# The second layer's long filters computed among the last four experts of the first layer

## The chip, the cores and the metric

The kernel runs on one core of a Trainium2 chip. Its time is the device time of one execution in microseconds (us); the median of three runs of the kernel before is 1987.41 us. TensorE is called PE here, VectorE DVE, ScalarE ACT, GpSimd POOL and SyncE SP.

## What is computed

A trunk of two layers over 256 tokens of width 1024, all in float32. A layer is a mixer and a mixture of experts:

```python
xn = rms_norm(x, norm1_w[l]); cols = xn @ w_in[l]
attn = mla_branch(...)                       # 16 heads
hy = hyena_branch(cols[..., COL_HYENA:COL_GATE], feats, tau, ...)
gates = sigmoid(cols[..., COL_GATE:])
merged = gates[:, :, 0] * (attn @ w_attn_branch[l]) + gates[:, :, 1] * (hy @ w_hyena_branch[l])
x = x + merged @ w_out[l]
x = x + expert_choice_ffn(rms_norm(x, norm2_w[l]), router_w[l], ...)   # 16 experts, 32 tokens each
```

The long filters of the Hyena branch do not depend on `x`, only on weights and positions, and this is what the change uses:

```python
h = sin(fr1 * (feats @ w1 + b1)); h = sin(fr2 * (h @ w2 + b2))
h = (h @ w3).reshape(L, 2, 1024) * exp(-tau * |deltas|)
h = h / sum(|h|, axis=0);  h_spec = rfft(h, n=2 * S, axis=0)
z = parts[0]
for n in range(2): z = parts[n + 1] * long_conv(z, h_spec[:, n], skip[n])
```

## The kernel before, in words

The program is written by hand for each engine; its order is the order of the code, and semaphores alone join the engines. Layers are `L` 0 and 1, experts `e` 0 to 15.

**Memory.** `ring` (22,528 columns of 4 bytes on 128 partitions) and `region` hold weights. In the mixer the ring has five slots (`SLOT_AT`) for 17 dense *units* of 2 MB: unit 0 the key and value up-projection, 1 to 6 the columns of the Hyena branch, 7 to 10 the gates, 11 to 14 the branch projections, 15 and 16 `w_out`. Units 14 to 16 lie in `R`, the first 12,288 columns of `region`. `m1` takes the latent weights, `m2` those of the query up-projection. In the experts the weights of one come in three transfers: A (6.5 MB: `w_gate` and the first part of `w_up`), B (5.0 MB: the rest of `w_up`) and D (5.8 MB: `w_down`). A has two areas (`wg_a`), one at the top of the ring and one in `region`, used by even and odd experts; B and D have one area each.

**SP** (`block.sync`) issues nearly all transfers in one queue. A transfer waits until the reader of what lies in its place is done: A waits for `gate_a` (the gate product of the expert two before, and one block of its up product), B for `up_done` and D for `o_psum` of the expert before. Whatever stands behind a waiting transfer waits too. ACT issues a few small loads in a queue of its own.

**PE in an expert** (`group`, L839): the gate product (L866), the up product (L866) in bank 3, transposes (L900, L906), the down product (L919), and four products (L937) that take the result to its tokens. In between ACT computes silu and DVE multiplies.

**The long filters** are computed in the mixer of each layer. The hidden layers (PE L519 and L537, DVE `sine_argument`, ACT Sin) lie in the query up-projection (L530). Behind the attention, between products for the gates (`next_gates`, L569), PE computes for each quarter `it` of the filters `filter_time` (L632, two products), `filter_spectrum` (L645, four) and `filter_sum` (L655, four). DVE (`decayed`), ACT (`abs_h`, `odd_filter`) and POOL take part in each. Then z is transposed (L669) and taken to its spectrum (`to_spectrum`, L681).

Of the kernel before, what the change touches and what calls it, by code (L numbers as in the profile page):

```python
# [51 lines left out]
NU, RING, RING_UNITS = 17, 5, 14  # L52
SLOT_AT = (0, 4096, 9856, 13952, 18176)
SLOT = DB * FF
# [11 lines left out]
def unit_slot(n):  # L66
    return (n + 4) % RING
# [7 lines left out]
UNITS_IN_SLOT = [sum(unit_slot(n) == s for n in range(RING_UNITS)) for s in range(RING)]  # L75
# [33 lines left out]
def build(nc, x, vecs, fvecs, qkw_in, consts_in, decay_in, w_lat, w_q_b, units_in,  # L109
          filt12, filt3, w_ga, w_gbu, w_down, w_down_last, out):  # L110
    with ExitStack() as ctx:
# [38 lines left out]
        w3 = R[:, 8192:8192 + 2048]  # L150
        w12 = R[0:64, 10240:10432]
        h2T = R[:, 10432:10432 + P]
        h1T = R[0:64, 10688:10688 + S]
        rr = R[0:64, 10944:10944 + 768]
        habs = R[:, 10688:11712]
        spec = R[:, 0:8192].rearrange("p (n b c) -> p n b c", n=2, b=4)
# [7 lines left out]
        decay = region[:, 12 * 1024:12 * 1024 + 2048].rearrange("p (b c) -> p b c", b=SB)  # L164
        hflt = W[:, 0:2048].rearrange("p (h b c) -> p h b c", h=2, b=SB)
# [49 lines left out]
        m2 = ring[:, M2AT:M2AT + QB * NH * QK].rearrange("p (i c) -> p i c", i=QB)  # L215

        def unit(n):
            if n >= RING_UNITS:
                return R[:, (n - RING_UNITS) * UNIT:(n - RING_UNITS + 1) * UNIT]
            a = SLOT_AT[unit_slot(n)]  # L220
            return ring[:, a:a + UNIT]

        def unit8(n):
            return unit(n).rearrange("p (i c) -> p i c", i=DB)

        wkv = unit(0).rearrange("p (i c) -> p i c", i=KVB)
# [8 lines left out]
        names = """one_dve half_dve consts_in dft_in vec_in fvec_in qkw_in filt_in decay_in wqb_in wgbu_in wga_third_in wga_last_in wu_tail_in out_done  # L235
# [16 lines left out]
        unit_in = [sem(f"unit_in{i}") for i in range(RING)]  # L252
        late_in = [sem(f"late_in{i}") for i in range(NU - RING_UNITS)]
# [4 lines left out]
        def _(sp):  # L258
            for L in range(DEPTH):
# [13 lines left out]
                if L == 0:  # L273
                    for t in range(SB):
                        sp.dma_start(x3[:, t], x[0, t * P:(t + 1) * P]).then_inc(x_in[t], 16)
                else:
                    sp.wait_ge(s["post_dve"], L * 4 + FREE)
                    sp.dma_start(vec[:, :], vecs[L]).then_inc(s["vec_in"], 16)
# [6 lines left out]
                sp.dma_start(unit(1), units_in[L, 1]).then_inc(unit_in[unit_slot(1)], 16)  # L285
                sp.dma_start(m2, w_q_b[L].rearrange("(i p) c -> p i c", p=P)).then_inc(s["wqb_in"], 16)
                sp.dma_start(unit(0), units_in[L, 0]).then_inc(unit_in[unit_slot(0)], 16)
# [5 lines left out]
                sp.dma_start(fvec[:, :], fvecs[L]).then_inc(s["fvec_in"], 16)  # L293

                def load_gate_a(e):
                    sp.dma_start(wg_a[e % 2], w_ga[L * E + e]).then_inc(wga_in[e % 2], 16)
# [28 lines left out]
                for n in range(2, RING_UNITS):  # L325
                    if n == 3:
                        sp.wait_ge(s["q_psum"], (L + 1) * 6)
                    if n >= RING:
                        unit_is_used(n - RING)
                    sp.dma_start(unit(n), units_in[L, n]).then_inc(unit_in[unit_slot(n)], 16)  # L330
                for k, (reader, count) in enumerate((("prod_dve", 2), ("prod_dve", 4), ("prod_dve", 4))):
                    sp.wait_ge(s[reader], L * 4 + count)
                    sp.dma_start(unit(RING_UNITS + k), units_in[L, RING_UNITS + k]).then_inc(late_in[k], 16)


                unit_is_used(9)
                unit_is_used(10)
# [9 lines left out]
                for b in range(FB):  # L347
                    unit_is_used(RING_UNITS + b)
# [7 lines left out]
                load_gate_a_second(12 * 1024 + SPARE, REGION - 3072)  # L356
                for e in range(1, E):
# [6 lines left out]
                    elif e < E - 2:  # L364
                        sp.wait_ge(s["gate_a"], L * E + e)
                        load_gate_a(e + 1)
                    elif e == E - 1:
# [3 lines left out]
                    if e == E - 2:  # L371
# [3 lines left out]
                    if e < E - 1:  # L375
                        load_down(e)
                    else:
# [11 lines left out]
        def _(pool):  # L389
            for L in range(DEPTH):  # L390
# [25 lines left out]
                for it in range(4):  # L416
                    pool.wait_ge(s["habs_act"], L * 4 + it + 1)
                    nc.gpsimd.tensor_tensor(habs[:, 0:HW], habs[:, 0:HW], habs[:, HW:2 * HW],
                                            ALU.add).then_inc(s["habs_pool"], 1)
# [3 lines left out]
        def _(pe):  # L423
# [3 lines left out]
            def unit_arrived(L, n):  # L427
                if n >= RING_UNITS:
                    pe.wait_ge(late_in[n - RING_UNITS], 16 * (L + 1))
                else:  # L430
                    pe.wait_ge(unit_in[unit_slot(n)], 16 * (L * UNITS_IN_SLOT[unit_slot(n)] + n // RING + 1))

            for n in ("gate_done", "up_done", "o_psum"):
                pe.sem_inc(s[n], FREE)
            def unread(count):
                for _ in range(count):
                    mm(bank(7, S), late[:, 0:P], late[:, 0:S], start=True, stop=True)

            pe.wait_ge(s["half_dve"], 1)
            unread(5)  # L440
            for L in range(DEPTH):
# [57 lines left out]
                def half_block(b, k):  # L499
                    n, j = 1 + b // 4, b % 4  # L500
                    for i in range(4 * k, 4 * k + 4):
                        m = mm(bank(b % 2, S), unit8(n)[:, i, j * P:(j + 1) * P], xnT[:, i],  # L502
# [7 lines left out]
                for i in range(5):  # L510
# [6 lines left out]
                pe.wait_ge(s["dft_in"], 16)  # L517
                pe.wait_ge(s["filt_in"], 48 * (L + 1))
                mm(bank(7, S), w12[0:33, 0:P], cst[0:33, C_FEAT:C_FEAT + S],  # L519
                   start=True, stop=True).then_inc(s["filt_psum"], 1)  # L520
# [4 lines left out]
                for g in range(6):  # L525
# [3 lines left out]
                    for i in range(QB):  # L529
                        m = mm(bank((3 + g) % 7), latT[:, i, t * P:(t + 1) * P], m2[:, i, c * 512:(c + 1) * 512],  # L530
                               start=i == 0, stop=i == QB - 1)
                    m.then_inc(s["q_psum"], 1)
                    if g == 1:

                        pe.wait_ge(s["consts_in"], 16)
                        pe.wait_ge(s["sin_act"], 2 * L + 1)
                        mm(bank(7, S), w12[:, 64:64 + P], h1T, start=True, stop=True).then_inc(s["filt_psum"], 1)  # L537

                unit_arrived(L, 0)
                for g in range(8):  # L540
# [26 lines left out]
                def gate_product(i, g, dst):  # L567
                    for k in range(DB):
                        m = mm(dst, unit8(7 + 2 * (i // 4) + g)[:, k, i % 4 * P:(i % 4 + 1) * P], xnT[:, k],  # L569
# [54 lines left out]
                def filter_time(it):  # L624
                    n, c = it // 2, it % 2
                    if it == 0:
                        pe.wait_ge(s["sin_act"], 2 * L + 2)
                    else:
                        pe.wait_ge(s["h_dve"], L * 4 + it)
                    for t in range(SB):  # L630
                        k = slice(64 * t, 64 * (t + 1))
                        m = mm(bank(t), h2T[k], w3[k, n * D + c * HW:n * D + (c + 1) * HW], start=True, stop=True)  # L632
# [1069 lines left out]
```

## Time and profile before

| | us |
|---|---|
| median of 3 runs (lowest, highest) | 1987.41 (1987.09, 1988.1) |
| span of the profiled execution, first to last instruction | 1985.9 |
| mixer of layer 1 and up to the first expert's end | 0 to about 411 |
| experts of layer 1 | about 411 to 996 |
| mixer of layer 2 and up to the first expert's end | about 996 to 1398 |
| experts of layer 2 | about 1398 to 1986 |
| PE busy (share of the span) | 1565.1 (79%) |
| DVE, ACT, POOL busy | 564.8, 289.5, 45.7 |
| bytes over the span | 644.37 MB, mean 324 GB/s |

The span leaves 1.5 us of the median outside. In both mixers PE is busy without a break and the DMA engines are partly idle; in the experts it is the other way round: the transfers come back to back and PE waits for them twice in each expert. The granted clock of TensorE is full in the mixers and 0.8 on average in the experts.

### The profile page before, as it was taken

To read this page: it belongs to the slowest core of one execution; us is meant where nothing else is said; L and a number is where in the kernel's file an instruction comes from. 1 tells how busy PE (TensorE), PEld (TensorE's weight loads), DVE (VectorE), ACT (ScalarE), POOL (GpSimd) and SP (SyncE) were. 2 spreads that over 40 slices of the span, in tenths; PEclk is the share of its full clock that TensorE was granted. 3 is DMA by queue.
4 is the path that set the end of the run, shared out by engine and by line. 5 is a ranking of instruction groups with operands and counts; after the bars stand their busy time and mean duration, and the time that the engine had idled before them with its cause. 6 is when DMAs were issued, how large, how long until landed. Compare 5 with 4: busy or idle time off the path is not lost.

```text
span 1985.9 us, 22283 instructions
## 1 busy us (share of the span) xinstructions
PE 1565.1 (79%) x9646; PEld 876.6 (44%) x9646; DVE 564.8 (28%) x1108; ACT 289.5 (15%) x610; POOL 45.7 (2%) x24
## 2 busy tenths in 40 slices
PE   9999999876665666576799999999766566666767
PEld 6687688532221232132267877885222222222322
DVE  3654772211111111111136547712111112111211
ACT  3233210210000000000032432102100000000010
POOL 0300000000000000000002000000000000000000
PEclk9999999998877887788899999998888778877888
DMA  8622055699999999999956221546999999999998
GB/s 296 233 86 85 1 226 214 252 417 434 431 428 438 428 433 433 429 433 425 426 209 233 85 85 44 235 178 271 439 427 432 435 430 431 431 433 432 430 430 343
DMA packets 26987, 644.37 MB, mean 324 GB/s; under 512 B 2960, under 2 KB 3984, under 8 KB 6672
## 3 DMA queue, kind: packets, MB, share of 16 engines
q1 hardware_dynamic: 25840, 638.47, 76.4%
q10 hardware_dynamic: 1056, 4.53, 0.8%
q8 instruction: 76, 1.25, 0.3%
q14 instruction: 15, 0.12, 0.0%
HBM read 641.94 MB, written 1.05 MB: 324 GB/s over the span
## 4 chain that ended last, share of the span: by engine, by line
DMA 49%; PE 48%; DVE 1%; DVEq 1%; issue 1%; ACT 0%; SPq 0%; ACTq 0%
DMA region<-w_down_dram 44%; PE ps L919 11%; PE ps L502 7%; PE ps L569 6%; PE ps L709 6%; DMA region<-w_down_last_dram 3%; PE ps L767 3%; DMA consts<-consts_dram 2%; PE ps L530 2%; PE ps L692 1%; PE ps L645 1%; PE ps L592 1%; PE ps L547 1%; PE ps L681 1%; PE ps L866 1%; PE ps L616 1%
## 5 line engine op out<-in xcount | busy, mean ns | idle before, releaser
L866 PE MATMUL ps<-ring,region 128*32 128x384 f32 (+1 forms) x2944 | 297.1, 538 | 190.9 <-DMA ring<-w_gbu_dram 190.9
L919 PE MATMUL ps<-region,late 128*32 128x512 f32 x1320 | 215.8, 777 | 157.7 <-DMA region<-w_down_dram 156.5
L866 PEld LDWEIGHTS ps<-ring,region 128*32 128x32 f32 x2944 | 122.2, 124 | 359.7 <-DMA ring<-w_gbu_dram 211.7
L919 PEld LDWEIGHTS ps<-region,late 128*32 128x32 f32 x1320 | 57.5, 138 | 295.1 <-issue 293.4
L502 PE MATMUL ps<-xnT,ring 128*128 128x256 f32 x768 | 178.3, 380 | 4.3 <-DVE region L1209 2.6
L1570 DVE TENSOR_TENSOR region<-region,ps 128x256 f32<-128x256 f32 x32 | 13.5, 421 | 543.7 <-PE ps L866 543.7
L502 PEld LDWEIGHTS ps<-xnT,ring 128*128 128x128 f32 x768 | 140.6, 190 | 23.9 <-DVE region L1209 4.4
L937 PE MATMUL ps<-region 128*128 128x512 f32 x256 | 123.8, 615 | 24.0 <-issue 22.4
L1581 DVE COPY region<-ps 128x512 f32<-128x512 f32 x32 | 22.1, 692 | 358.8 <-PE ps L919 358.1
L569 PE MATMUL ps<-xnT,ring 128*128 128x256 f32 x512 | 115.8, 380 | 0.0
L1584 DVE TENSOR_TENSOR x<-x,ps 128x512 f32<-128x512 f32 x128 | 88.0, 687 | 76.3 <-PE ps L937 76.3
L569 PEld LDWEIGHTS ps<-xnT,ring 128*128 128x128 f32 x512 | 95.9, 190 | 18.2 <-issue 6.3
L866 PE MATMUL ps<-region 128*32 128x384 f32 (+1 forms) x1152 | 96.1, 463 | 0.3 <-DMA region<-w_ga_dram 0.2
L937 PEld LDWEIGHTS ps<-region 128*128 128x128 f32 x256 | 40.9, 188 | 109.5 <-issue 66.7
L1180 ACT ACT_TABLE_LOAD x30 | 38.5, 1283 | 329.2 <-PE ps L866 329.2
L709 PE MATMUL ps<-region,ring 128*128 128x256 f32 x384 | 84.5, 379 | 0.0
L1189 ACT ACTIVATE region<-ps 128x512 f32<-128x512 f32 x32 | 19.1, 597 | 405.6 <-PE ps L919 392.1
L709 PEld LDWEIGHTS ps<-region,ring 128*128 128x128 f32 x384 | 72.8, 190 | 9.8
L866 PEld LDWEIGHTS ps<-region 128*32 128x32 f32 x1152 | 41.7, 109 | 55.8 <-issue 49.1
L1184 ACT ACTIVATE region<-ps 128x256 f32<-128x256 f32 x32 | 12.3, 384 | 364.0 <-PE ps L900 364.0
L767 PE MATMUL ps<-region 128*128 128x512 f32 x128 | 56.4, 593 | 0.0
L1061 ACT ACTIVATE region<-ps,small 128x256 f32<-128x256 f32 x64 | 29.8, 470 | 84.4 <-DVE small L1363 84.4
(207 smaller groups left out, 1478.1 us busy)
## 6 DMA issues: line engine op xcount, KB each, us to landing
region<-w_down_dram SPq DMA_DIRECT2D x28, 5632.0 KB, 32.5
ring<-w_gbu_dram SPq DMA_DIRECT2D x30, 4928.0 KB, 33.3
region<-w_ga_dram SPq DMA_DIRECT2D x12, 6336.0 KB, 37.1
ring<-w_ga_dram SPq DMA_DIRECT2D x12, 6336.0 KB, 34.7
ring<-units_dram SPq DMA_DIRECT2D x28, 2048.0 KB, 8.6
region<-units_dram SPq DMA_DIRECT2D x6, 2048.0 KB, 11.8
region<-w_ga_dram SPq DMA_DIRECT2D x2, 4928.0 KB, 32.1
ring<-w_ga_dram SPq DMA_DIRECT2D x2, 4288.0 KB, 13.6
```

The lines of the kernel that those rows point to most:

```text
L502: m = mm(bank(b % 2, S), unit8(n)[:, i, j * P:(j + 1) * P], xnT[:, i], start=i == 0, stop=i == DB - 1)
L530: m = mm(bank((3 + g) % 7), latT[:, i, t * P:(t + 1) * P], m2[:, i, c * 512:(c + 1) * 512], start=i == 0, stop=i == QB - 1)
L569: m = mm(dst, unit8(7 + 2 * (i // 4) + g)[:, k, i % 4 * P:(i % 4 + 1) * P], xnT[:, k], start=k == 0, stop=k == DB - 1)
L709: m = mm(bank(2 * (i % 2) + 1, S, g * S), unit8(n)[:, k, j * P:(j + 1) * P], (uT if g else aT)[:, k], start=k == 0, stop=k == DB - 1)
L767: m = mm(bank(4 + 2 * t + c), mT[:, k, t * P:(t + 1) * P], unit8(15 + c)[:, k], start=k == 0, stop=k == DB - 1)
L866: m = mm(bank(b, QW[j], rows=CAP, row0=CAP * j), xs[:, i, q * CAP:(q + 1) * CAP], w[i][:, j * FT:j * FT + QW[j]], start=i == 0, stop=i == ...
L919: m = mm(bank(c, rows=CAP, row0=CAP * j), hT[:, b * P + CAP * j:b * P + CAP * (j + 1)], wd[:, CT * b + j, c * 512:(c + 1) * 512], start=b ...
L937: mm(bank(6 + k % 2), gselT[:, t * P:(t + 1) * P], o_sb[:, c * 512:(c + 1) * 512], start=True, stop=True).then_inc(s["y2_psum"], 1)
L1061: m = af(p_t[:, h % 2, t], bank(3 + h % 2, S, t * S), ACT.Exp, bias=nmax[:, c:c + 1], accum_out=rsum[:, c:c + 1])
L1180: af(sil[:, 0:2 * P], bank(2, 2 * P), ACT.Silu)
L1581: copy(o_sb[:, 512:1024], bank(1)).then_inc(s["o_dve"], 1)
L1584: tt(xc, xc, bank(6 + k % 2), ALU.add).then_inc(s["x_dve"], 1)
```

## The change

Layer 1 keeps its filters where they were. Those of layer 2 are computed while the experts 12 to 15 of layer 1 run, in seven steps `k` (`filter_ahead`): 0 and 1 are the hidden layers, steps 2 to 5 begin with `filter_time(k - 2)`, steps 3 to 6 have `filter_spectrum` and `filter_sum` of quarter `k - 3`. On PE an even step lies behind the gate product, before the first block of the up product, and an odd step behind the transposes, before the down product. Expert 12 has steps 0 and 1, 13 has 2 and 3, 14 has 4 and 5, and 15 has 6.

```diff
+                        if last and L < DEPTH - 1:
+                            filter_ahead(L + 1, ahead[0], n)
                         pe.wait_ge(s["hid_dve"], n + FREE)
-                        product(3, wu[q % 2], 0).then_inc(s["gate_a"], 1)
+                        product(3, wu[home], 0).then_inc(s["gate_a"], 1)
...
+                        if last and L < DEPTH - 1:
+                            if q < GROUP - 1:
+                                filter_ahead(L + 1, ahead[1], n)
+                            filter_banks_read(L + 1, min(ahead[1], 6))
                         pe.wait_ge(s["hT_dve"], n + 1)
...
+            def filter_ahead(L, k, n):
+                if k == 0:
+                    pe.wait_ge(s["x_dve"], n * 4 + X_FREE)
+                if k < 2:
+                    filter_hidden(L, k)
+                    return
+                if k < 6:
+                    if k >= 4:
+                        pe.wait_ge(s["spec_dve"], L * 12 + 3 * (k - 4) + 2)
+                    filter_time(L, k - 2)
+                if k >= 3:
+                    it = k - 3
+                    pe.wait_ge(s["x_dve"], n * 4 + X_FREE)
+                    filter_spectrum(L, it, 0, 6)
+                    if k < 6:
+                        pe.wait_ge(s["h_dve"], L * 4 + it + 2)
+                    filter_spectrum(L, it, 1, 0)
+                    pe.wait_ge(s["gselT_act"], n + k % 2)
+                    filter_sum(L, it, 4, S)
+            def filter_banks_read(L, k):
+                if k == 1:
+                    pe.wait_ge(s["arg_dve"], 2 * L + 2)
+                else:
+                    pe.wait_ge(s["spec_dve"], L * 12 + 3 * (k - 3) + 2)
```

On DVE the even step stands before the multiplication that the down product needs, and on ACT four experts are now written out behind the loop. ACT loads what the filters need in its own queue: the hidden weights (48 KB) and `vec` (64.5 KB) once the rows of the last group are picked, the output weights (512 KB) and the decay (1024 KB) in expert 12. Before, these loads but `vec` were made in the mixer, with the output weights twice.

```diff
 # DVE, group
+                        if last and L < DEPTH - 1:
+                            filter_ahead(L + 1, 2 * q)
                         dve.wait_ge(s["sil_act"], n + 1 + FREE)
                         dve.wait_ge(s["up_done"], n + 1 + FREE)
 # DVE, filter_ahead, step 0
+                if k == 0:
+                    dve.wait_ge(s["vec_in"], 16 * (L + 1))
 # ACT, behind the loop over twelve experts
+                    act.wait_ge(s["xs_psum"], 4 * NG * (L + 1))
+                    act.wait_ge(s["post_dve"], (L + 1) * 4 + FREE)
+                    load_filter_hidden(L + 1)
+                    act.dma_start(vec[:, :], vecs[L + 1]).then_inc(s["vec_in"], 16)
 # ACT, expert 12, behind silu
+                        filter_ahead(L + 1, ahead[0])
+                        if ahead[0] == 0:
+                            act.wait_ge(s["gate_a"], n + 1)
+                            load_filter_out(L + 1)
+                            load_decay(L + 1)
```

The filters and their spectra lie in the upper part of the ring. So from expert 13 of layer 1 on there is one area for A, that in `region`:

```diff
-                    elif e < E - 2:
+                    elif e < (E - 2 if last_layer else E - 3):
                         sp.wait_ge(s["gate_a"], L * E + e)
                         load_gate_a(e + 1)
...
                     if e < E - 1:
                         load_down(e)
+                        if not last_layer and e >= E - 3:
+                            sp.wait_ge(s["gate_a"], L * E + e + 1)
+                            load_gate_a(e + 1)
```

The mixer of layer 2 has three slots of the ring for its units, and three places in `R`; the query weights lie in `region`.

```diff
+UNIT_HOMES = ((4, 0, 1, 2, 3, 4, 0, 1, 2, 3, 4, 0, 1, 2, 5, 6, 7),
+              (1, 0, 2, 1, 0, 2, 1, 0, 2, 5, 6, 1, 0, 2, 5, 6, 7))
+UNIT_ORDER = ((2, 3, 4, 5, 6, 7, 8, 9, 10, 11, 12, 13, 14, 15, 16),
+              (2, 3, 4, 5, 6, 7, 8, 11, 9, 10, 12, 13, 14, 15, 16))
```

SP's queue at the end of layer 1 and the start of layer 2, from B of expert 13 on, before:

```order
L299 DMA ring<-w_gbu_dram 128x9856 [waits up_done]
L319 DMA region<-w_down_dram 128x11264 [waits o_psum]
L299 DMA ring<-w_gbu_dram 128x9856 [waits up_done]
L312 DMA region<-w_ga_dram 128x2816 [waits gate_a]
L319 DMA region<-w_down_dram 128x11264 [waits o_psum]
L312 DMA region<-w_ga_dram 128x9856
L316 DMA ring<-w_gbu_dram 128x5632 [waits up_done]
L316 DMA ring<-w_gbu_dram 128x4224
L380 DMA region<-w_down_last_dram 128x5632 [waits o_psum]
```

and now:

```order
L325 DMA ring<-w_gbu_dram 128x9856 [waits up_done]
L345 DMA region<-w_down_dram 128x11264 [waits o_psum]
L322 DMA region<-w_ga_dram 128x12672 [waits gate_a]
L325 DMA ring<-w_gbu_dram 128x9856 [waits up_done]
L345 DMA region<-w_down_dram 128x11264 [waits o_psum]
L322 DMA region<-w_ga_dram 128x12672 [waits gate_a]
L342 DMA ring<-w_gbu_dram 128x5632 [waits up_done]
L342 DMA ring<-w_gbu_dram 128x4224
L418 DMA region<-w_down_last_dram 128x5632 [waits o_psum]
```

A of expert 14, which stood ahead of these rows, now stands behind D of expert 13, and A of 15 is whole and behind D of 14. PE in the mixer of layer 2 behind the attention, before (L569 are the gates, L669 transposes z, L681 is the spectrum of z):

```order
L569 MATMUL ps<-xnT,ring 128x256 x8
L632 MATMUL ps<-region 128x512 x2
L569 MATMUL ps<-xnT,ring 128x256 x8
L632 MATMUL ps<-region 128x512 x2
L645 MATMUL ps<-region,consts 96x512 x4
L655 MATMUL ps<-consts,region 128x1 x4
...
L669 MATMUL ps<-consts,region 128x128 x8
L645 MATMUL ps<-region,consts 96x512 x4
L669 MATMUL ps<-consts,region 128x128 x8
L655 MATMUL ps<-consts,region 128x1 x4
L569 MATMUL ps<-xnT,ring 128x256 x8
L681 MATMUL ps<-region,consts 96x512 x4
```

and now (L680 the gates, L746 the transposes, L759 the spectrum of z):

```order
L680 MATMUL ps<-xnT,ring 128x256 x8
L746 MATMUL ps<-consts,region 128x128 x8
L680 MATMUL ps<-xnT,ring 128x256 x8
L746 MATMUL ps<-consts,region 128x128 x8
L680 MATMUL ps<-xnT,ring 128x256 x8
L759 MATMUL ps<-region,consts 96x512 x4
```

The four quarters of the filters are gone from here. Their products now stand in the experts; expert 13, behind its transposes (L994, L1000) and before its down product (L1017):

```order
L994 MATMUL ps<-consts,region 128x128 x2
L1000 MATMUL ps<-consts,region 128x128 x2
L1000 MATMUL ps<-consts,region 128x96
L503 MATMUL ps<-ring 128x512 x2
L515 MATMUL ps<-ring,consts 96x512 x4
L523 MATMUL ps<-consts,xnT 128x1 x4
L1017 MATMUL ps<-region,late 32x512 x22
```

where L1000 was followed by L1017 before.

## Rows read from the trace of the kernel before

**Rows 1.** The page: busy tenths and GB/s in 40 slices of the span
```profile
PE   9999999876665666576799999999766566666767
PEclk9999999998877887788899999998888778877888
GB/s 296 233 86 85 1 226 214 252 417 434 431 428 438 428 433 433 429 433 425 426 209 233 85 85 44 235 178 271 439 427 432 435 430 431 431 433 432 430 430 343
```

**Rows 2.** Chain of waits, end of layer 1: start, us, what
```profile
891.89 32.60 DMA region<-w_down_dram
...
960.61 27.64 DMA region<-w_down_last_dram
```

**Rows 3.** Chain of waits, layer 2 behind the attention
```profile
1179.52 1.06 PE ps L632 x4
...
1185.29 3.60 PE ps L645 x8
1188.89 0.79 PE ps L655 x8
...
1201.62 3.43 PE ps L645 x8
1205.06 0.95 PE ps L669 x8
...
1206.79 3.56 PE ps L569 x16
1210.35 3.43 PE ps L681 x8
```

**Rows 4.** Windows: busy us of each engine, granted clock, DMA share, GB/s
```profile
1175.00:1215.00 40.00, 40.00 (x167) 23.94 (x164) 20.19 (x39) 15.09 (x22) 5.05 (x4) 1.00 0.04 19
```

**Rows 5.** Timeline, PE, query up-projection of layer 2
```profile
1025.42 5.39 PE L530 MATMUL ps<-ring,region 128*128 128x512 f32 x12 [0.18 <-ACT region L1027]
1030.79 0.67 PE L537 MATMUL ps<-region 64*128 64x256 f32 x2
```

**Rows 6.** DMA issues from 995 to 1062 us: size of one, us to landing
```profile
ring<-units_dram SPq DMA_DIRECT2D x3, 2048.0 KB, 7.5
region<-filt_dram ACTq DMA_DIRECT2D x2, 512.0 KB, 14.0
region<-decay_dram ACTq DMA_DIRECT2D x1, 1024.0 KB, 4.8
region<-filt_dram ACTq DMA_DIRECT2D x1, 48.0 KB, 8.9
```

**Rows 7.** Timeline, PE, expert 12 of layer 1
```profile
860.95 6.01 PE L866 MATMUL ps<-ring,region 128*32 128x384 f32 x72
871.20 6.41 PE L866 MATMUL ps<-ring,region 128*32 128x384 f32 x56 [4.25 <-DMA ring<-w_gbu_dram]
884.62 7.23 PE L919 MATMUL ps<-region,late 128*32 128x512 f32 x44 [5.67 <-DMA region<-w_down_dram]
892.60 3.86 PE L937 MATMUL ps<-region 128*128 128x512 f32 x8 [0.75 <-issue]
```

**Rows 8.** Timeline, DVE, first sine argument of layer 2, its first and last row
```profile
1027.09 0.53 DVE L1217 TENSOR_SCALAR region<-ps,vec 64x256 f32<-64x256 f32 x1
...
1029.90 0.28 DVE L1228 TENSOR_SCALAR region<-region 64x256 f32<-64x256 f32 x1
```

**Rows 9.** Timeline, SP's queue: issues of B and of D of expert 13
```profile
877.68 0.33 SPq L299 DMA_DIRECT2D ring<-w_gbu_dram  x1
891.89 0.33 SPq L319 DMA_DIRECT2D region<-w_down_dram  x1
```

**Rows 10.** Timeline, PE: expert 14 without a wait; the first down product of layer 2
```profile
936.87 10.52 PE L866 MATMUL ps<-ring,region 128*32 128x384 f32 x128
...
1397.75 5.35 PE L919 MATMUL ps<-region,late 128*32 128x512 f32 x44 [0.62 <-DVE late L1574]
```

**Rows 11.** Timeline, PE, last products of layer 1
```profile
988.28 1.92 PE L945 MATMUL ps<-region,late 128*32 128x512 f32 x16 [0.34 <-DMA region<-w_down_last_dram]
993.91 1.98 PE L937 MATMUL ps<-region 128*128 128x512 f32 x4 [0.80 <-DVE region L1581]
```

**Rows 12.** Timeline, SP, layer 2: A and B of the first expert
```profile
1281.76 0.33 SPq L302 DMA_DIRECT2D ring<-w_ga_dram  x1
1309.49 0.33 SPq L299 DMA_DIRECT2D ring<-w_gbu_dram  x1
```

More of the change, by code:

```diff
@@ L51 @@
 UNIT = DB * 512
[L52 removed]
 SLOT_AT = (0, 4096, 9856, 13952, 18176)
+RING = len(SLOT_AT)
+ROWS_HOMES = 3
 SLOT = DB * FF
@@ L414, in _ @@
                     ALU.mult).then_inc(s["qkr_pool"], 1)
[L416 to L419, printed above, removed]
+                if L == 0:
+                    sum_of_halves(0)
+                if L < DEPTH - 1:
+                    sum_of_halves(L + 1)
         @block.tensor
@@ new lines, in filter_time @@
+            def filter_time(L, it):
+                n, c = it // 2, it % 2
+                if it == 0:
+                    pe.wait_ge(s["filt3_in"], 32 + 16 * L)
+                    pe.wait_ge(s["sin_act"], 2 * L + 2)
+                else:
+                    pe.wait_ge(s["h_dve"], L * 4 + it)
+                for t in range(SB):
+                    k = slice(64 * t, 64 * (t + 1)) if L == 0 else slice(0, 64)
+                    h = h2T[L][k] if L == 0 else h2T[L][:, t * P:(t + 1) * P]
+                    m = mm(bank(t), h, w3[L][k, n * D + c * HW:n * D + (c + 1) * HW], start=True, stop=True)
+                m.then_inc(s["f3_psum"], 1)
@@ new lines, in basis, with filter_spectrum @@
+            def basis(par, f):
+                a = C_F + (2 * par + f) * NK
+                return cst[:, a:a + NK]
+            def filter_spectrum(L, it, f, bank0):
+                pe.wait_ge(s["h_dve"], L * 4 + it + 1)
+                if it >= 1:
+                    pe.wait_ge(s["spec_dve"], L * 12 + 3 * (it - 1) + f + 1)
+                for par in range(2):
+                    m = mm(bank(bank0 + par, rows=NK), basis(par, f), hflt[L][it % 2][:, par], start=True, stop=True)
+                m.then_inc(s["dft_psum"], 1)
@@ new lines, in filter_sum @@
+            def filter_sum(L, it, b, off):
+                pe.wait_ge(s["habs_pool"], L * 4 + it + 1)
+                if it >= 1:
+                    pe.wait_ge(s["spec_dve"], L * 12 + 3 * it)
+                for j in range(4):
+                    m = mm(bank(b, 1, off + j), habs[L][:, j * P:(j + 1) * P], ones, start=True, stop=True)
+                m.then_inc(s["hsum_psum"], 1)
+            def filter_ahead(L, k, n):
[17 more added lines that the diff above has]
+                    filter_sum(L, it, 4, S)
@@ L1214, in sine_argument @@
                 dve.wait_ge(s["filt_psum"], 2 * L + k + 1)
-                a, turns, rest = (rr[:, i * S:(i + 1) * S] for i in range(3))
+                a, turns, rest = (rr[L][:, i * S:(i + 1) * S] for i in range(3))
                 c = V_FB1 + 2 * k
```

419 lines of the change are left out of this document (241 added, 178 removed).

## The prediction

> **What bounds the kernel now.** I read the slices first [rows 1]. In slices 1 to 7 and 21 to 27, the mixers, PE stands at 9 and the DMA engines move 1 to 250 GB/s in most slices; in the other slices they move 425 to 438 GB/s and PE stands at 6 or 7. So the mixers are PE's and the experts are the transfers'. The chain of waits says the same: it goes from each D to the next [rows 2], 40 us for an expert. An expert's 17.3 MB at 432 GB/s take 40.1 us: A 15.0, B 11.7, D 13.4. In the mixer of layer 2 the chain is PE alone, and in the stretch of the filters PE is busy for 40.00 of 40 us at full clock, while DVE has 20.19 and the DMA engines 4% [rows 3, 4]. PE time taken from there should come off the end, as nothing else is near to full. PE time added to the experts should cost nothing until PE is late with freeing a weight area that the next transfer waits for, and bytes added there cost in full.
>
> **What is taken away.** The filters' products go from the chain of layer 2 [rows 3]: four times L632 at 1.06 (4.2), four times L645, three at 3.60 and one at 3.43 (14.2), four times L655 at 0.79 (3.2): 21.6 us. Checked the other way: from 1179.52 to 1210.35 there are 30.8 us, of which two gate products (3.65 and 3.56) and two transposes (1.05 and 0.95) stay, 9.2; again 21.6. ACT and POOL wait for nothing new there, and DVE's next work is released by L681, which moves along. The hidden layers: L537 stands between back-to-back products, and its chain share is 0.6; L519 was hidden, as L530 behind it waited for ACT anyway [rows 5]. Together **-22.2 us**. Layer 1's mixer computes the same in the same order: 0.
>
> **What is added in bytes.** 48, 512 and 1024 KB move from a stretch with idle DMA engines to one that has none: 1.62 MB at 432 GB/s, **+3.7 us**. `vec` (64.5 KB) was already loaded there.
>
> **What is moved in the experts.** Here a wait can appear, and I follow the clock of the profile through expert 12.
> - ACT issues the two small loads when the rows of the last group are picked, at about 861 [rows 7]. Each gives a DMA engine 4 and 8 rows, and each engine still has SP's rows of some 45 KB, 1.7 us each at 27 GB/s. The same 48 KB load took 8.9 us among SP's smaller rows, more than the 1024 KB decay took alone (4.8) [rows 6]; so such a load does not overtake. If one of SP's rows goes between every two, 12 rows need 20 us and start-up, and `vec` lands at about 884.5. The bounds: 8.9 us as measured (871), and the end of all that SP has queued, A no longer among it (897).
> - By the Trainium skill (DMA: Bandwidth & Descriptors, Queues, rings and completion order) an engine drains a whole packet of typically 9 to 17 descriptors before it turns to another ring. The two loads would then stand behind the rest of B and behind D of expert 12, and `vec` would land at 885 and the sum grow by about 0.5 us; no row before shows the order of single packets.
> - DVE waits for `vec` before the first sine argument, and the multiplication for the down product is queued behind it. An argument takes 3.1 us [rows 8]: 887.6. Multiplication, transposes and ACT's sine take it to about 890.5; the second hidden product (0.7) and the second argument, for which PE waits (`filter_banks_read`), take it to 894.7. The down product of expert 12 then starts at 895 in place of 884.62, and is cold as before (7.2 us): 902.3. So D of expert 13 is issued at 902.3 in place of 891.89 [rows 9].
> - Without A of expert 14, which the change moves behind it, the DMA engines have at that time only B of 13 (884.5 + 11.7) and ACT's 3.7 us: they run dry at 899.9. With 2 us from issue to data (a unit lands 7.5 us after issue for 4.9 us of bytes [rows 6], 2.6 for both ends) D flows from 904.3. **+4.4 us** idle. The bounds are 0 (`vec` before 880) and 15 (`vec` at 897 and a cold PE).
> - Expert 13: tokens 4.6, gate product and first block 6.0 [rows 7], step 2 1.1: 914. A of 14 is issued then, data from 916, and D ends at 917.7. 1.7 us to spare, so the single area for A costs 0 here, but only just. I take **+0.5**.
> - Step 3 has 5.5 us of products [rows 3] and some 1.6 us of hand-overs to ACT and DVE; up product 4.6 and down product 5.35 at full clock [rows 10]. D of 14 is issued at 933 and needed at 942, A of 15 at 950 and needed at 956. No wait of the transfers.
> - Expert 15: A lands at 973 and PE is free at 973.5; gate 5.3, step 6 4.4, up 5.3, hand-overs 3.2: the last down product starts at 991.5, when its first part lands. What follows is set by the last parts, as before: the chain ends in a transfer and two token products [rows 2, 11]. PE has about 2 us to spare, the only slack from here back to the start of expert 13's down product.
>
> **Layer 2's dense units.** Three slots serve while a slot is read for 12 us or more and a unit lands in 7.5 us [rows 6]: 0. The query weights are last in the first batch and need `o_psum` of the last expert; I have them 20 us after it, with L530 30 us after it. Units 9 and 10 land some 16 us after the attention, with 20 us to spare. Units 14 to 16 now wait for the last gate product and take 14.6 us, A of the first expert (before at 1281.76) another 10, and B is due at 1309.49 [rows 12]: 25 of 27.7 us. Costs 0; the gap that covers it is nearly used up.
>
> **Sum.** -22.2 + 3.7 + 4.4 + 0.5 = -13.6. From the span of 1985.9: 1972.3. The median is 1.5 us above the span, so the runs should give **1974 us**. A measurement of this kernel can tell about 0.2%, 4 us, from no change.
>
> **The rivals.**
> - *All side work hidden* (chance 0.20). `vec` lands early, as 8.9 us would have it, and only the bytes cost: 1987.4 - 22.2 + 3.7 = 1969. For it: the load is small. Against: rows 6.
> - *Long hand-overs* (0.14). Steps 3 to 6 have each two or three turns PE to ACT to DVE and back; 2 us more in each of four steps are 8, less the 2 of slack: 1980. The bank and table switches there are in no row before.
> - *A late load in layer 2* (0.05). If the query weights or units 14 to 16 are 10 us later than I have them, PE stands still in the mixer: 1984.
> - *The single area at half clock, slower than before* (0.06). PE's products in experts 13 to 15 could run at 1.2 GHz, as the down product of 12 does (7.2 against 5.35 us [rows 7, 10]). Steps 3 to 6 have about 21 us of products, which would take as much again; what is beyond the 2 us of slack goes to the end: 1974 + 19 = 1993. It decides from 15 us on. For it: the granted clock is 0.8 on average in the experts. Against: PE is cold there since it waits for B and D; from expert 13 on both are there before PE asks, and expert 14 of the kernel before, which waits for nothing, runs 128 products in 10.52 us. The Trainium skill (TensorE: Matmul & The Clock Gate, The HAM clock gate) has half the clock as the default, released by activity, which speaks for this rival only where PE stands still.
> - That the saving is none, because something other than PE holds layer 2, has nothing for it [rows 4].
>
> **How the numbers follow.** My forecast has 0.55. Of its cases all are faster by over 0.2% (below 1983.4), and so are the first two rivals; the third lies within 0.2% or just beyond. Faster 0.87, same 0.07, slower 0.06. The range goes from below the first rival, 1967, to beyond the second, 1982; the last two rivals and the tail of the bound of 15 us are left out.
>
> **What would show it.** In the profile after: the stretch between the attention and the first spectrum of z in layer 2 is 9 us, not 31; layer 1 ends some 8 us later; B of 13 and D of 13 have a gap of about 4 us of idle DMA between them and DVE's sine argument waits for a transfer into `vec`; the down product of expert 12 starts near 895; L1017 in experts 13 and 14 takes 5.4 us. Wrong: a DMA gap in front of A of 14 or of 15, half-clock products in steps 3 to 6, or PE waiting for units in layer 2.

## The result and the profile after

| | us (lowest, highest) | runs |
|---|---|---|
| before, same chip | 1987.74 (1987.09, 1988.1) | 4 |
| the change | 1975.55 (1974.04, 1978.51) | 4 |

The ratio is 0.994, 95% interval 0.9928 to 0.9952: 12.2 us less, where 13.4 were predicted. The profiled execution is the slowest of the four (span 1976.1, its run 1978.51); the other three have spans of 1972.2 to 1974.0. So some numbers of this profile are up to 4 us on the late side, and I give a second profile of the same kernel (`c1_change_again`, span 1972.5) where that matters. The slices, which answer to [rows 1]:

```profile
PE   9999999876655675658989999998757566556767
PEclk9999999998878787788999999999988788887888
GB/s 298 232 88 86 1 220 222 254 410 429 428 434 430 433 430 436 426 394 393 432 325 85 86 105 188 106 305 266 433 437 432 430 431 431 431 437 431 430 426 342
```

PE is fuller in slices 19 and 20, the last experts of layer 1 (8 and 9 tenths for 6 and 7), and in slices 18 and 19 the transfers fall to 394 and 393 GB/s, the one place among layer 1's experts where they are disturbed.

**Layer 2 gained what was forecast.** Timeline of PE behind the attention, for the stretch of [rows 3]:

```profile
1191.12 1.11 PE L746 MATMUL ps<-consts,region 128*128 128x128 f32 x8
1192.07 3.62 PE L680 MATMUL ps<-xnT,ring 128*128 128x256 f32 x16
1195.52 1.11 PE L746 MATMUL ps<-consts,region 128*128 128x128 f32 x8
1196.47 3.62 PE L680 MATMUL ps<-xnT,ring 128*128 128x256 f32 x16
1199.93 3.60 PE L759 MATMUL ps<-region,consts 128*96 128x512 f32 x8
```

From 1191.12 to the first spectrum of z at 1199.93 there are 8.8 us, where there were 30.8. Taken from the last product of layer 1 to the end of the span, it is 1976.1 - 1008.5 = 967.6 us, and was 1985.9 - 995.9 = 990.0: -22.4 for a forecast of -22.2.

**Layer 1 gave part of it back.** Its last products, which answer to [rows 11]:

```profile
994.39 2.77 PE L1043 MATMUL ps<-region,late 128*32 128x512 f32 x22 [2.16 <-DMA region<-w_down_last_dram]
999.20 3.62 PE L1043 MATMUL ps<-region,late 128*32 128x512 f32 x16 [2.04 <-DMA region<-w_down_last_dram]
...
1006.52 1.98 PE L1035 MATMUL ps<-region 128*128 128x512 f32 x4 [0.80 <-DVE region L1750]
```

The end of layer 1 moved from 995.9 to 1008.5, by 12.6 us (forecast 8.6). -22.4 + 12.6 is the whole difference of the spans, -9.8. The same rows in the second profile:

```profile
997.43 1.92 PE L1043 MATMUL ps<-region,late 128*32 128x512 f32 x16 [2.04 <-DMA region<-w_down_last_dram]
...
1003.06 1.98 PE L1035 MATMUL ps<-region 128*128 128x512 f32 x4 [0.80 <-DVE region L1750]
```

There the end moved by 9.1 us, and the products that the last transfer releases take 1.92 instead of 3.62: the granted clock from 999 to 1003 was 0.57 in the first profile, so mostly 1.2 GHz, and 1.00 (2.4 GHz) from 997.4 to 999.4 in the second.

Where it went is seen in expert 12. Timeline of PE, for [rows 7]:

```profile
861.77 5.36 PE L952 MATMUL ps<-ring,region 128*32 128x384 f32 x64
874.68 1.19 PE L486 MATMUL ps<-consts,xnT 33*128 33x256 f32 x2 [7.55 <-DMA xnT<-filt_dram]
875.80 7.33 PE L952 MATMUL ps<-ring,region 128*32 128x384 f32 x64
...
889.09 0.85 PE L1000 MATMUL ps<-consts,region 128*128 128x128 f32 x3 [5.59 <-DVE region L1738]
889.87 1.22 PE L491 MATMUL ps<-xnT 64*128 64x256 f32 x2
894.27 8.32 PE L1017 MATMUL ps<-region,late 128*32 128x512 f32 x44 [3.19 <-DVE xnT L1374]
```

DVE stood still for `vec`, as forecast:

```profile
885.40 0.53 DVE L1363 TENSOR_SCALAR xnT<-ps,vec 64x256 f32<-64x256 f32 x1 [22.58 <-DMA vec<-vecs_dram]
```

and SP's queue, for [rows 9]:

```profile
883.20 0.33 SPq L325 DMA_DIRECT2D ring<-w_gbu_dram  x1
902.65 0.33 SPq L345 DMA_DIRECT2D region<-w_down_dram  x1
915.26 0.33 SPq L322 DMA_DIRECT2D region<-w_ga_dram  x1
...
933.96 0.33 SPq L345 DMA_DIRECT2D region<-w_down_dram  x1
950.96 0.33 SPq L322 DMA_DIRECT2D region<-w_ga_dram  x1
...
971.36 1.28 SPq L418 DMA_DIRECT2D region<-w_down_last_dram  x3
```

There are two waits. One I had not priced: PE stands 7.55 us for the 48 KB of hidden weights and runs the up product at 7.33 us, the slow kind. So B of expert 13 is issued at 883.20, not at 877.68 [rows 9]. The other is the forecast one: the down product starts at 894.27 (forecast 895), and D of 13 is issued at 902.65 (902.3). The windows show what the DMA engines did in 5 us each; the last two columns are their busy share and their GB/s:

```profile
875.00:880.00 5.00, 5.00 (x33) 2.05 (x35) 0.00 (x0) 0.00 (x0) 0.00 (x0) 0.52 0.86 369
880.00:885.00 5.00, 3.50 (x40) 1.24 (x32) 0.00 (x0) 0.00 (x0) 0.00 (x0) 1.00 0.70 238
...
890.00:895.00 5.00, 1.81 (x6) 0.57 (x10) 3.14 (x8) 0.52 (x2) 0.00 (x0) 0.50 1.00 358
895.00:900.00 5.00, 5.00 (x28) 1.18 (x24) 0.00 (x0) 0.00 (x0) 0.00 (x0) 0.50 0.91 255
900.00:905.00 5.00, 4.24 (x24) 1.18 (x16) 1.20 (x2) 0.60 (x1) 0.00 (x0) 0.97 1.08 354
```

The gap before B of 13 is plain (share 0.70). Behind 890 it is different: the engines are busy, but move only 358, 255 and 354 GB/s. Something that flows there is slow. ACT issues the 512 KB at 888.54 and the decay at 889.07. Over the experts 12 to 15 (845 to 1000) the mean is 405 GB/s and was 427: 3.4 MB, or 7.9 us at 432 GB/s, are missing, and with the added 3.7 us of bytes that is 11.6 of the 12.6 us by which layer 1's end moved. Issues from 860 to 905, size and us to landing:

```profile
ring<-decay_dram ACTq DMA_DIRECT2D x1, 1024.0 KB, 16.0
ring<-filt_dram ACTq DMA_DIRECT2D x1, 512.0 KB, 14.5
vec<-vecs_dram ACTq DMA_DIRECT2D x1, 64.5 KB, 23.0
xnT<-filt_dram ACTq DMA_DIRECT2D x1, 48.0 KB, 12.7
```

### The profile page after: what moved, and what is told of

It reads as the page before. It is cut to its first block, busy times and chain, and to the rows that moved or that the text cites. A ratio compares the mean times of both kernels' runs of the same rounds, so it can differ in the third digit from the quotient of the medians.

```text
span 1976.1 us, 22283 instructions
## 1 busy us (share of the span) xinstructions
PE 1564.4 (79%) x9646; PEld 876.0 (44%) x9646; DVE 566.1 (29%) x1108; ACT 283.3 (14%) x604; POOL 45.8 (2%) x24
## 3 DMA queue, kind: packets, MB, share of 16 engines
HBM read 641.42 MB, written 1.05 MB: 325 GB/s over the span
## 4 chain that ended last, share of the span: by engine, by line
PE 50%; DMA 45%; DVE 2%; issue 1%; DVEq 1%; ACT 0%; SPq 0%; ACTq 0%
DMA region<-w_down_dram 40%; PE ps L1017 11%; PE ps L617 7%; PE ps L680 6%; PE ps L787 6%; PE ps L853 3%; DMA region<-w_down_last_dram 3%; PE ps L952 2%; DMA consts<-consts_dram 2%; PE ps L643 2%; PE ps L770 1%; PE ps L703 1%; PE ps L658 1%; PE ps L759 1%; PE ps L515 1%; DMA vec<-vecs_dram 1%
## 5 line engine op out<-in xcount | busy, mean ns | idle before, releaser
L952 PE MATMUL ps<-ring,region 128*32 128x384 f32 (+1 forms) x2872 | 287.8, 534 | 174.9 <-DMA ring<-w_gbu_dram 174.9
L1017 PE MATMUL ps<-region,late 128*32 128x512 f32 x1320 | 218.0, 785 | 145.7 <-DMA region<-w_down_dram 138.9
L1017 PEld LDWEIGHTS ps<-region,late 128*32 128x32 f32 x1320 | 57.5, 140 | 285.6 <-issue 277.4
L617 PE MATMUL ps<-xnT,ring 128*128 128x256 f32 x768 | 178.3, 380 | 4.3 <-DVE region L1355 2.6
L617 PEld LDWEIGHTS ps<-xnT,ring 128*128 128x128 f32 x768 | 140.6, 190 | 23.9 <-DVE region L1355 4.4
L1750 DVE COPY region<-ps 128x512 f32<-128x512 f32 x32 | 22.1, 692 | 342.5 <-PE ps L1017 341.9
L952 PE MATMUL ps<-region 128*32 128x384 f32 (+1 forms) x1224 | 102.7, 463 | 0.0
L680 PE MATMUL ps<-xnT,ring 128*128 128x256 f32 x384 | 86.8, 380 | 0.0
L680 PEld LDWEIGHTS ps<-xnT,ring 128*128 128x128 f32 x384 | 71.9, 190 | 13.5 <-issue 4.6
```

The lines of the kernel that those rows point to most:

```text
L617: m = mm(bank(b % 2, S), unit8(L, n)[:, i, j * P:(j + 1) * P], xnT[:, i], start=i == 0, stop=i == DB - 1)
L680: m = mm(dst, unit8(L, 7 + 2 * (i // 4) + g)[:, k, i % 4 * P:(i % 4 + 1) * P], xnT[:, k], start=k == 0, stop=k == DB - 1)
L952: m = mm(bank(b, QW[j], rows=CAP, row0=CAP * j), xs[:, i, q * CAP:(q + 1) * CAP], w[i][:, j * FT:j * FT + QW[j]], start=i == 0, stop=i == ...
L1017: m = mm(bank(c, rows=CAP, row0=CAP * j), hT[:, b * P + CAP * j:b * P + CAP * (j + 1)], wd[:, CT * b + j, c * 512:(c + 1) * 512], start=b ...
L1750: copy(o_sb[:, 512:1024], bank(1)).then_inc(s["o_dve"], 1)
```

## The experiments

The loss (9.6 us by medians: the 22.1 of `e7_no_filters` below, less the 12.5 of `c1_change_again`, each against the kernel before that stood beside it) has four candidates: the waits for the small loads, the added bytes, PE's products in the experts, and the single area for A. Theory A of the quotes is my sum: mostly the waits. The kernel before stood beside each batch: 1987.85 for c1 and e1 to e3, 1988.47 for e4 to e7, 1987.64 for the others. Differences are of medians; with each taken against the kernel before of its own batch they shift by up to 0.7. All but e4, e7, p1 and p2 are edits of the changed kernel.

**c1: the change again.** 

> The changed kernel once more, beside the three edits of it that follow. All theories: 1975.5 us within 2, and layer 1's last token products (L1035) end 10 to 13 us later than before.

1975.38 us, ratio 0.9939 (0.9926 to 0.9953). The result repeats. Layer 1 ends 9.1 us later than before in its profile, not 10 to 13. Where a profile of the change is compared with another run below, this one is the fairer.

**e1: `vec` before the twelve experts.**

```diff
+                    act.wait_ge(s["post_dve"], (L + 1) * 4 + FREE)
+                    act.dma_start(vec[:, :], vecs[L + 1]).then_inc(s["vec_in"], 16)
                     with act.Fori(0, SPARE_FROM) as e:
...
                     load_filter_hidden(L + 1)
-                    act.dma_start(vec[:, :], vecs[L + 1]).then_inc(s["vec_in"], 16)
```

> ACT loads vec of layer 2 ahead of the experts of layer 1; the 48 KB of hidden weights stay where the change has them. Theory A (the experts lose time because PE and DVE wait for the two small loads, which come late among SP's large rows): DVE's first sine argument starts when PE gives it (about 875), the down product of expert 12 at about 888 in place of 894, but PE still waits for the hidden weights until about 874 and B of expert 13 is issued late; 1972.5 us (1971 to 1974). Theory B (the added products and hand-overs, or the single area for A, cost the time): 1975.5. Theory C (only the bytes count, the waits are hidden): 1975.5.

1974.92, ratio 0.9933 (0.992 to 0.9947): not different from c1, a miss for A. The down product of expert 12 starts at 888.17, as expected, and D of 13 is issued at 896.17, 4.4 us earlier than in c1. Nearly nothing of that reaches the end: the last part lands only 1.6 us earlier (its 16 products start at 995.84, in c1 at 997.43), and these products take 3.59 us here and 1.92 there, so that layer 1 ends at 1005.1 in both profiles.

**e2: both small loads early.** The hidden weights go to a place that is free (`qkw`).

```diff
-        w12 = (R[0:64, 10240:10432], xnT_t[0:64, 0:192])
+        w12 = (R[0:64, 10240:10432], qkw[0:64, 0:192])
...
                     act.wait_ge(s["post_dve"], (L + 1) * 4 + FREE)
+                    load_filter_hidden(L + 1)
+                    act.dma_start(vec[:, :], vecs[L + 1]).then_inc(s["vec_in"], 16)
+                    with act.Fori(0, SPARE_FROM) as e:
+                        expert(e, False)
```

> Both small loads ahead of the experts of layer 1; the hidden weights of layer 2 go to the tile of qkw, which is free there. Theory A: no wait for either; B of 13 is issued at 878 and D of 13 by 893, no idle DMA engines, only the 3.7 us of bytes stay: 1969 us (1967 to 1970.5). Theory B and theory C: 1975.5.

1974.43, ratio 0.9932 (0.9918 to 0.9945), where A had 1969. Both waits are gone, and 1 us is gained. PE's timeline of e2 says what stands in their place:

```profile
889.26 8.10 PE L1017 MATMUL ps<-region,late 128*32 128x512 f32 x44 [9.90 <-DMA region<-w_down_dram]
```

D of expert 12, there at 884.62 in the kernel before [rows 7], now lands at 889. Its windows:

```profile
870.00:875.00 5.00, 3.93 (x34) 1.86 (x37) 1.34 (x4) 0.42 (x1) 0.00 (x0) 0.66 1.01 433
875.00:880.00 5.00, 3.91 (x37) 1.56 (x29) 1.68 (x4) 0.39 (x1) 0.00 (x0) 1.00 1.04 327
880.00:885.00 5.00, 0.00 (x0) 0.00 (x0) 2.11 (x6) 0.42 (x1) 0.00 (x0) 0.62 0.98 278
885.00:890.00 5.00, 0.74 (x4) 0.23 (x8) 0.00 (x0) 0.00 (x0) 0.00 (x0) 0.50 1.04 424
```

No gap (shares 1.04 and 0.98), and yet 327 and 278 GB/s in the 10 us that begin 3.4 us behind the issue of the 512 KB at 871.61. When the 1024 KB of the decay flow behind them, the rate is back at 424. The packets of e2, summed by queue (`--dma` with a window), say the same: from 875 to 884.4 an engine moves, while busy, 17.7 GB/s in ACT's rows and 18.8 in SP's beside them; from 884.4 to 902 it is 25.5 and 25.9. The queue and the size of the rows are the same in both stretches, and SP's large rows lie between them in both, so it is neither the second queue nor the mixing of small rows with large ones. So the slow loads and the waits overlap in the change: part of the slow stretch lies in time that the waits had lost already. That is my reading of why taking the waits away gives so little.

**e3: only the hidden weights early.** Their place is `qkw` as in e2, and `vec` stays where it was.

```diff
+                    act.wait_ge(s["post_dve"], (L + 1) * 4 + FREE)
+                    load_filter_hidden(L + 1)
                     with act.Fori(0, SPARE_FROM) as e:
...
-                    load_filter_hidden(L + 1)
                     act.dma_start(vec[:, :], vecs[L + 1]).then_inc(s["vec_in"], 16)
```

> Only the hidden weights early, vec stays late. Theory A: B of 13 is issued in time (878), but DVE still waits for vec until about 885 and the down product of expert 12 starts at about 894; the first gap of the DMA engines goes, a second of 3 to 4 us comes in front of D of 13: 1974 us (1972.5 to 1975.5). If the wait for the hidden weights alone were the cost, 1969; if neither counts, 1975.5.

1972.93, ratio 0.9925 (0.9911 to 0.9938), within what was expected, but not by the path expected: without the 48 KB ahead of it `vec` takes 17.6 us and lands near 878, not 885, the down product of expert 12 starts at 887.11, not 894, and of the second gap only a share of 0.86 in one window of 5 us is seen. Its median is 2.5 us below c1, but the intervals overlap.

**e4: the single area alone,** on the kernel before.

```diff
+        def second_home(L, e):
+            return e % 2 == 1 or (L < DEPTH - 1 and e == E - 2)
...
-                    elif e < E - 2:
+                    elif e < (E - 2 if last_layer else E - 3):
...
+                        if not last_layer and e >= E - 3:
+                            sp.wait_ge(s["gate_a"], L * E + e + 1)
+                            load_gate_a(e + 1)
```

> The kernel before with one part of the change alone: one area for A from expert 13 of layer 1 on, in SP's new order; filters and units as before. Theory A: A of 14 and of 15 are issued before the DMA engines run dry, no cost: ratio 1.000 (within 1 us). Theory B (the single area is what costs): 3 to 9 us slower than before.

1987.96, ratio 0.9995 (0.9986 to 1.0004). The single area costs nothing that can be measured.

**e5: few bytes.** e2, with 1/32 of the output weights and of the decay loaded for layer 2.

```diff
-                        act.dma_start(w3[M][64 * t:64 * (t + 1)], filt3[M]).then_inc(s["filt3_in"], 16)
+                        act.dma_start(w3[M][64 * t:64 * (t + 1), 0:(2048 if M == 0 else 64)], filt3[M][:, 0:(2048 if M == 0 else 64)]).then_inc(s["filt3_in"], 16)
...
-                    act.dma_start(decay[M], decay_in).then_inc(s["decay_in"], 16)
+                    act.dma_start(decay[M] if M == 0 else decay[M][:, :, 0:32], decay_in if M == 0 else decay_in[:, :, 0:32]).then_inc(s["decay_in"], 16)
```

> As e2_both_early, but the output weights and the decay of layer 2 are loaded only in 1 of 32 parts of their columns (the rest of the filters is computed from what lies there). Prices the bytes: the 1.57 MB at the rate of the experts are 3.6 us, so 3.5 us faster than e2_both_early (about 1965). If the small rows cost more than their bytes, 5 to 6 us faster; if they are hidden, the same as e2_both_early.

1967.33, ratio 0.9896 (0.9881 to 0.9911): 7.1 us less than e2 (7.7 against the kernel before of each), more than any of the three cases expected, where the bytes at 432 GB/s are 1.52 MB, 3.5 us. The two intervals together leave about 3 to 11 us for this difference, so the medians alone don't exclude the bytes' price; the rates in the windows are the firmer evidence. The same windows as in e2 read:

```profile
875.00:880.00 5.00, 4.45 (x44) 1.74 (x34) 1.20 (x4) 0.38 (x1) 0.00 (x0) 1.00 1.08 430
880.00:885.00 5.00, 0.00 (x0) 0.00 (x0) 2.58 (x7) 0.42 (x1) 0.00 (x0) 0.66 0.95 408
```

In e2 these 10 us moved 302 GB/s on average: 10 x (1 - 302 / 432) = 3.0 us lost. 3.5 + 3.0 is 6.5 of the 7.1. The run prices the 512 KB and the decay together, and not each.

**e6: the spectrum products twice.** e2 with 14.4 us of PE work more in experts 13 to 15:

```diff
-                for par in range(2):
+                for par in (range(2) if L == 0 else (0, 1, 0, 1)):
```

> As e2_both_early, with every product of filter_spectrum of layer 2 computed twice: 3.6 us more of PE in each of steps 3 to 6. Theory A has PE time in experts 12 to 15 hidden while the transfers are ahead: with both small loads early the slack at the last expert is 2 us and the 4 to 8 us regained, so of the 14.4 us some 5 to 8 come through. If PE were the bound there, all 14.4; if PE time is free, none.

1980.81, ratio 0.9967 (0.9955 to 0.9979): 6.4 us more than e2. PE's work in the experts of e2 is hidden, with some 8 us to spare.

**e7: the kernel before without layer 2's filters,** neither loads nor products nor DVE's and ACT's part:

```diff
-                filter_time(0)
...
-                filter_sum(3)
+                if L == 0:
+                    filter_time(0)
...
+                else:
+                    z_transposed(0)
+                    next_gates()
+                    z_transposed(1)
```

> The kernel before without any long filters in layer 2: their products, sines and loads are left out, and the spectra are what lies in their place. Prices what the change takes from the mixer: 22.2 us faster than before (1965.5), and 9 us from the attention to the first spectrum of z. If DVE or ACT hold the mixer behind it, less: 15 to 20 us.

1966.39, ratio 0.989 (0.9875 to 0.9906): -22.1 us, for a forecast of -22.2. This is what a perfect hiding place would give.

**p1 and p2: what extra bytes cost in either queue.** The kernel before, with 640 KB of constants (128 partitions, rows of 5 KB) loaded four times more in layer 1's experts, by ACT or by SP:

```diff
+                        if e in (4, 6, 8, 10):
+                            act.wait_ge(s["dft_in"], 8 * e - 16)
+                            act.dma_start(cst[:, C_F:C_N], consts_in[:, C_F:C_N]).then_inc(s["dft_in"], 16)
```

> The kernel before, with 4 loads of 640 KB (constants that it has already) added among the experts of layer 1 in ACT's queue. 2.62 MB at 432 GB/s are 6.1 us. Theory M (small rows of one queue that run between the large rows of the other slow both, so that the change's 1.57 MB cost 7 us): 10 to 12 us slower than before. Theory N (bytes cost their bytes, the rest was waits): 6 us slower.

> The same 4 loads in SP's queue, where they stand behind one another with the weights. Theory M: 6 us slower than before, since nothing runs between. Theory N: 6 us too. If small rows are slow by themselves: 10 to 12.

1994.0, ratio 1.0035 (1.0021 to 1.0049), and 1995.55, ratio 1.0039 (1.0025 to 1.0053): +6.4 and +7.9 us for 2.62 MB, which are 6.1 us at 432 GB/s. Theory M, that a second queue in itself costs more than its bytes, falls: while one of p1's loads flows (613 to 628) the DMA engines move 433 to 445 GB/s.

**e8 and e9: the 512 KB and the decay in SP's queue,** ahead of B of expert 13; e8 is e2 with this, e9 the change with this.

```diff
+                    if not last_layer and e == E - 3:
+                        sp.wait_ge(s["gate_a"], L * E + e)
+                        sp.dma_start(w3[1][0:64], filt3[1]).then_inc(s["filt3_in"], 16)
+                        sp.dma_start(decay[1], decay_in).then_inc(s["decay_in"], 16)
```

> As e2_both_early (both small loads ahead of the experts), with the output weights and the decay in SP's queue, ahead of B of expert 13. Theory M: only their bytes are left, 3.6 of the 7.1 us: 1971 us (1969.5 to 1972.5), faster than both kernels. Theory N: 1974.4, as e2_both_early.

> The change, with the output weights and the decay in SP's queue ahead of B of 13; the two small loads stay late. Theory M: the slow mixed stretch goes, the waits for the small loads now show in full, as idle DMA engines in front of B and D of 13: 1973 (1971.5 to 1975). Theory N: 1975.4.

e8: 1972.92, ratio 0.9933 (0.9919 to 0.9947), 1.5 below e2 and just outside the range of theory M; the interval, 1971.5 to 1977.1 us, reaches into that range and over theory N's value, so that the time decides neither. e9: 1978.44, ratio 0.9951 (0.9937 to 0.9964), 3.0 above the change where less was expected: a miss, though the intervals of e9 and c1 overlap. The windows of e8 show the slow stretch in SP's queue too:

```profile
875.00:880.00 5.00, 3.64 (x29) 1.33 (x21) 1.92 (x5) 0.38 (x1) 0.00 (x0) 0.96 1.05 351
880.00:885.00 5.00, 0.00 (x0) 0.00 (x0) 1.85 (x6) 0.42 (x1) 0.00 (x0) 0.72 0.97 227
885.00:890.00 5.00, 2.86 (x16) 0.90 (x20) 0.00 (x0) 0.00 (x0) 0.00 (x0) 0.50 0.94 301
```

So it goes with the load, not with the queue. The decay flows beside the 512 KB there, so that this run can't tell the two apart.

The slow stretch follows the issue of the 512 KB wherever that lies: it is issued at 878.92 in e1, where 880 to 890 shows 226 and 345 GB/s; at 881.38 in e3, with 295 and 242 from 885 to 895; and at 876.97 in e9, with 381, 225 and 244 from 875 to 890. In e4, where these loads are still in the mixer, no 5 us from 850 to 915 move under 372. The kernel before has it too, in layer 2's mixer: two loads of 512 KB, one for each half of the partitions, are issued from 1000.8 to 1002.1, and from 1005 to 1015 the engines move 272 and 232 GB/s at shares of 1.02 and 1.05.

In e9 the slow stretch lies before `vec` has landed: 26.5 us after its issue, at 888.3, where c1 has 884.7. So D of 13 is issued at 904.01 (c1: 900.52), and what had been a gap before B of 13 is now one before D of 13, with 355 and 141 GB/s at shares of 0.82 and 0.36 from 895 to 905. From there on every transfer of SP is 3.5 us later than in c1, up to the last D (974.41 for 970.93): this is the 3 us.

## Why the prediction was right, and where its terms were off

The median came out 1.5 us above the 1974 predicted, and inside the range; what layer 2 gives and the wait for `vec` came as forecast. The term that was mis-sized is that of the bytes, "1.62 MB at 432 GB/s, **+3.7 us**". By medians, with c1 for the change:

| term, us | forecast | measured |
|---|---|---|
| layer 2 without the filters | -22.2 | -22.1 (e7) |
| the large loads | +3.7 | +7.1 (e5 against e2) |
| waits for the small loads, the single area, the rest | +4.9 | +2.5 (what is left of the 9.6 given back) |
| sum | -13.6 | -12.5 |

Two errors nearly cancel, and that they do is luck. The split between the two is that of e2 and e5, where nothing waits for the small loads; in the change, where delays lie over one another, it isn't sharp.

- **The bytes** were mis-sized by about two, by the medians. The 512 KB of output weights are 64 rows of 8 KB into 64 partitions. While they flow, the DMA engines show a share near 1 and 227 to 351 GB/s for 10 to 15 us, in ACT's queue (e2) and in SP's (e8). The decay of e2, rows of 8 KB too but into 128 partitions, and the constants of p1, 128 partitions, flow at or near full rate. [Rows 6] had it in them: 14.0 us for 512 KB and 4.8 for 1024 KB, and I read them only for how long a small load takes. The Trainium skill (SBUF — State Buffer, Door 1: The DMA port swizzle) says that partitions 0 to 63 reach only 8 of the 16 ports by which transfers write, and gives them half the rate, about 218 GB/s. It says so of a load by itself; the windows here mix the load with others, which are slowed too (18.8 for 25.9 GB/s in SP's rows of e2). That the 64 partitions are the cause fits all these rows, but is not shown, as it was not tried: the test would be the same 512 KB spread over 128 partitions. That the load is slow to read where it lies in memory would fit as well.
- **The waits.** For `vec` the times were right at every step: landing 885.4 for 884.5, down product 894.27 for 895, D of 13 at 902.65 for 902.3, D of 14 at 933.96 for 933, A of 15 at 950.96 for 950. (In c1 D of 13 is issued at 900.52, so such a match is closer than two runs of the kernel agree.) The rule behind it holds: from 865.7 to 872.5 the DMA engines take 75 packets of SP's queue and 75 of ACT's, one for one. The wait of PE for the 48 KB load was missed, although it stands in the same queue and first; it moved B of 13 by 5.5 us and so turned the forecast gap before D of 13 into one before B of 13. Together the engines idled for less than the forecast 4.4 us: shares of 0.86, 0.70, 0.88 and 0.91 in four windows of 5 us are 3.3 us. And part of that time covers the slow load.
- **The single area** costs nothing (e4; forecast 0.5). The mean DMA share from 910 to 1000 is 0.99.
- **PE in the steps** ran at full clock, and the down product waits 1.2 us for the last hand-over. L1017 took 5.35 us in expert 13 as forecast, but 7.05 in 14, where 5.4 was forecast: the granted clock was 0.77 there, so in part 1.2 GHz, though PE had been busy for 6.44 of the 6.70 us before its 1.2 us of waiting. The slack was more than my 2 us: of e6's 14.4 us 8 are hidden on top of the steps.
- **Layer 2's units** cost nothing: A of the first expert is issued at 1272.76 and B at 1299.22, 9.0 and 10.3 us earlier than in [rows 12], as the mixer is shorter.
- **The last parts.** I let the end move with the bytes. PE waits 2.16 and 2.04 us for them, where it waited 1.88 and 0.34 before [rows 11], and what the second releases ran at 3.62 us in one profile and 1.92 in the other. These 1.7 us can be part of the spread of the change's runs (4.5 us in four); that they make it, no run shows, as the kernel before spreads by up to 5.6 us (nine runs beside c1).

**The rivals.** All hidden (1969) fell: both its waits came. The long hand-overs fell, and so did the half clock: the products of `filter_spectrum` take 602 ns each in the experts and 599 in the mixer before. The late load in layer 2 did not come. That the saving is none fell with e7.

Is there a version that beats both? e3 (1972.93) and e8 (1972.92) have medians 2.5 us below the change, but their intervals reach into its own. What e5 points to, the 512 KB over all partitions, would be worth some 3 us by its windows, and wasn't tried.

## What to carry to other kernels

Work that moves into a transfer-bound stage pays for its loads, and the price need not be that of the bytes at the best rate: look in the trace how long the same load took elsewhere, and compare it with a larger one that took less. A small load issued in a stage whose DMA engines are full takes 13 to 27 us here (48 and 64.5 KB); issue it a stage early, and follow every engine that waits for it, the first in its queue too. And before a wait is taken away, ask what is slow beneath it: two delays in the same place do not add, and removing one shows the other.

## What the runs showed that was not expected

- Small loads beside a full queue: 48 KB took 12.7 us and 64.5 KB 23.0 to land, for 8.9 in [rows 6]. It is the rows that count, not the bytes. A load of 64 rows, 4 for each engine, lands after 12.7 us with 48 KB and after 12.5 with the 16 KB of e5; 8 rows need 17.6 (`vec` in e3), 12 need 23.0 (`vec` behind the 48 KB in the change), and e5's 32 KB, which are 256 pieces behind 64 rows, so 20 for each engine, need 35.6. From these times an estimate is 1.2 to 1.5 us for each row, where the prediction has 1.7 us for one of SP's rows.
- DVE and POOL. Timeline of the change, DVE and then POOL:

```profile
928.67 0.18 DVE L1403 RECIPROCAL small<-small 128x4 f32<-128x4 f32 x1
928.76 1.11 DVE L1404 TENSOR_TENSOR small<-small,vec 128x4 f32<-128x4 f32 x1
...
928.58 1.28 POOL L432 TENSOR_TENSOR xnT<-xnT 128x512 f32<-128x512 f32 x1 [10.32 <-ACT xnT L1133]
```

A DVE instruction on 128x4 takes 1.11 us and ends at 929.87, with POOL's (928.58 + 1.28 = 929.86). The same instruction takes 1.11 us beside POOL's in two more quarters (951.54 and 964.46), and 0.13 in the last (987.02), where POOL does nothing. The Trainium skill (SBUF — State Buffer, Who interferes with whom) says that a DVE instruction with two inputs in SBUF contends with a GpSimd instruction that reads SBUF, and the rows agree. Here it costs nothing that can be seen: DVE's next instruction starts at 933.97.
